# Hybrid decoder layer: the first weights' first half is loaded ahead of x's second tile, which PE turns between the first projection's products

## What is computed

```python
h = rms_norm(x, norm1_g[l])
proj = h @ w_in[l]                        # 1024 x 2856, thirteen pieces
(nq, nkc, nvc, nks, nvs, nkw, nvw, ngate, gq, gk, gv, glr, gr) = jnp.split(proj, split_points, axis=-1)
nsa_out = nsa_mixer(nq, nkc, nvc, nks, nvs, nkw, nvw, ngate, positions, ...)
gla_out = gla_mixer(gq, gk, gv, glr, gr, gla_w_gate[l], gla_b_gate[l], gla_norm_g[l])
x = x + jnp.concatenate([nsa_out, gla_out], axis=-1) @ w_out[l]
h2 = rms_norm(x, norm2_g[l])
x = x + moe_ffn(h2, w_router[l], b_router[l], w_gate_up[l], b_gate_up[l], w_down[l], b_down[l])
```

## Time and profile before

| what | value |
|---|---|
| runs | 1064.62, 1066.3, 1068.13 us, median 1066.3 |
| profiled execution | 1063.68 us, of which the span is 1061.9 us |
| PE busy in the span | 1017.3 us (96%) |
| DVE, ACT busy | 294.1 us, 168.1 us |
| HBM read | 424.83 MB, 401 GB/s over the span |
| granted TensorE clock, mean | 1.0 |

### The profile page before, as it was taken

How to read it: one execution, slowest core, us unless ns; L and a number is a source line. 1 busy time by engine, 2 the same in 40 slices (tenths; PEclk the granted TensorE clock), 3 DMA queues, 4 the chain that set the end, 5 groups by cost and what they waited for, 6 DMA issues and landing times.

```text
span 1061.9 us, 12030 instructions
## 1 busy us (share of the span) xinstructions
PE 1017.3 (96%) x4977; PEld 410.7 (39%) x4977; DVE 294.1 (28%) x681; ACT 168.1 (16%) x324; POOL 15.9 (1%) x42
## 2 busy tenths in 40 slices
PE   9999999999999999999999999999999999989998
PEld 5555644333333333333333333333333333333334
DVE  1664625222222222211222122222112222221222
ACT  2434322111111111100111011111101111110111
POOL 4100000000000000000000000000000000000000
PEclk9999999999999999999999999999999999999999
DMA  9992668999999999999999999999999999999997
GB/s 296 362 408 88 246 270 343 426 425 436 428 430 433 433 433 430 428 430 431 434 434 433 433 426 430 433 432 434 432 431 426 426 434 433 434 431 430 420 426 276
DMA packets 36023, 426.45 MB, mean 402 GB/s; under 512 B 3782, under 2 KB 12062, under 8 KB 19728
## 3 DMA queue, kind: packets, MB, share of 16 engines
q1 hardware_dynamic: 33952, 424.52, 95.0%
q0 software_dynamic: 704, 1.04, 0.5%
q10 hardware_dynamic: 1328, 0.33, 0.1%
HBM read 424.83 MB, written 1.05 MB: 401 GB/s over the span
## 4 chain that ended last, share of the span: by engine, by line
PE 62%; DMA 34%; DVE 2%; SPq 1%; issue 1%; ACT 0%; DVEq 0%
DMA pair<-in_w_down 30%; PE bank L1741 24%; PE bank L1753 14%; PE bank L1329 5%; DMA pair<-in_w_gate_up 4%; PE bank L1775 4%; PE bank L1604 3%; PE bank L1725 2%; PE bank L1767 2%; PE bank L1733 1%; PE bank L1760 1%; PE bank L1401 1%; PE bank L1969 1%; SPq L369 1%; PE bank L1361 1%; PE bank L1388 1%
## 5 line engine op out<-in xcount | busy, mean ns | idle before, releaser
L1741 PE MATMUL bank<-pair,xs 128*64 128x512 f32 x2048 | 450.1, 594 | 21.0 <-DMA pair<-in_w_gate_up 19.9
L1741 PEld LDWEIGHTS bank<-pair,xs 128*64 128x64 f32 x2048 | 143.0, 137 | 323.1 <-issue 286.9
L1753 PE MATMUL bank<-pair,sig 128*64 128x512 f32 x960 | 212.2, 593 | 14.2 <-DMA pair<-in_w_down 14.2
L1222 DVE COPY gu<-bank 128x512 f32<-128x512 f32 x32 | 36.9, 1154 | 415.3 <-PE bank L1741 415.3
L1753 PEld LDWEIGHTS bank<-pair,sig 128*64 128x64 f32 x960 | 72.3, 137 | 149.9 <-issue 143.8
L760 ACT COPY gu<-bank 128x512 f32<-128x512 f32 x32 | 36.9, 1152 | 458.1 <-PE bank L1741 458.1
L862 DVE TENSOR_TENSOR xs<-bank,gt 128x512 f32<-128x512 f32 x31 | 21.4, 691 | 221.0 <-PE bank L1733 221.0
L1329 PE MATMUL bank<-stage,xt 128*128 128x512 f32 x160 | 72.2, 598 | 0.0
L1775 PE MATMUL bank<-ys,pgt 64*128 64x512 f32 x248 | 61.6, 615 | 0.3 <-ACT ys L765 0.3
L1725 PE MATMUL bank<-xr,onehot 128*64 128x512 f32 x248 | 58.5, 592 | 0.0
L765 ACT COPY ys<-bank 128x512 f32<-128x512 f32 x31 | 18.2, 586 | 206.9 <-PE bank L1753 206.9
(11 more groups left out here) (316 smaller groups left out, 496.8 us busy)
## 6 DMA issues: line engine op xcount, KB each, us to landing
pair<-in_w_gate_up SPq DMA_DIRECT2D x51, 4096.0 KB, 39.7
pair<-in_w_down SPq DMA_DIRECT2D x24, 4096.0 KB, 37.9
pair<-in_w_gate_up SPq DMA_DIRECT2D x22, 2048.0 KB, 14.7
pair<-in_w_down SPq DMA_DIRECT2D x15, 1024.0 KB, 13.3
pair<-in_w_down SPq DMA_DIRECT2D x6, 2048.0 KB, 33.0
stage<-in_w_in SPq DMA_DIRECT2D x5, 2048.0 KB, 19.2
pair<-in_w_gate_up SPq DMA_DIRECT2D x8, 1024.0 KB, 4.9
stage<-in_w_out SPq DMA_DIRECT2D x2, 2048.0 KB, 15.6
```

Of the source, the lines that this page charges most:

```text
L1222: V.tensor_copy(gu[:, 1, :].rearrange("p (i q) -> p q i", i=FQ), up_banks[1][:].rearrange("p (q i) -> p q i", i=FQ)).then_inc(s["gu_lo"], 1)
L1741: last = mm(up_banks[a][b * CAP:(b + 1) * CAP, :].rearrange("p (q i) -> p q i", i=FQ), xs[:, k, :], cols[:, b], start=k == 0, stop=k == DK ...
L1753: last = mm(down_bank[b * CAP:(b + 1) * CAP, :], actf[:, kk % FQ, kk // FQ, :], row[:, 512 * b:512 * (b + 1)], start=kk == 0, stop=kk == D ...
```

## The change

SP issues x's first tile, then the first half of the first weights, then x's second tile, then the second half. PE no longer turns x's second tile ahead of the first product: it turns it behind the first four products (tile 0, k-tiles 0 to 3). The products then go (tile 0, low half), the turning of tile 1, (tile 0, high half), (tile 1, low half), (tile 1, high half). The turned gains go through bank 6 in place of bank 4. Nothing is added or left out; the number of instructions on every engine stays as it was.

```diff
         @block.sync
         def _(sp):
-            for ti in range(NT):
+            def rows_of_x(ti):
                 sp.dma_start(xr[:, ti, :], x[0, ti * P:(ti + 1) * P, :]).then_inc(s[f"xin{ti}"], 16)
+
+            rows_of_x(0)
...
                 if i == 0:
                     sp.dma_start(dst[:, 0:4, :], src[:, 0:4, :]).then_inc(s["w_low"], 16)
+                    rows_of_x(1)
                     dst, src = dst[:, 4:DK, :], src[:, 4:DK, :]
...
             dve.wait_ge(s["g1_full"], 1)
-            V.tensor_copy(gt2[:, 0:DK], banks[4][:, 0:DK]).then_inc(s["g1t"], 1)
+            V.tensor_copy(gt2[:, 0:DK], banks[6][:, 0:DK]).then_inc(s["g1t"], 1)
...
-            for ti in range(NT):
+            def x_turned(ti):
                 pe.wait_ge(s[f"xin{ti}"], 16)
...
-                if ti == 0:
-                    pe.wait_ge(s["grows1"], 16)
-                    tp(banks[4][:, 0:DK], grows[:], ident[0:DK, 0:DK]).then_inc(s["g1_full"], 1)
+
+            x_turned(0)
+            pe.wait_ge(s["grows1"], 16)
+            tp(banks[6][:, 0:DK], grows[:], ident[0:DK, 0:DK]).then_inc(s["g1_full"], 1)
...
-            for half in range(2):
+            def first_project(ti, half):
+                pe.wait_ge(s["xt"], 2 * ti + half + 1)
+                for k in range(4 * half, 4 * half + 4):
+                    last = mm(banks[PROJ_BANKS[ti]][:, 0:280 + RANK], xt[:, k, ti * P:(ti + 1) * P],
+                              front_slot(0)[:, k, :], start=k == 0, stop=k == DK - 1)
                 if half:
-                    front_arrived(pe, 0)
-                else:
-                    pe.wait_ge(s["w_low"], 16)
-                for ti in range(NT):
...
+                    last.then_inc(s["proj_full"], 1)
+
+            pe.wait_ge(s["w_low"], 16)
+            first_project(0, 0)
+            x_turned(1)
+            front_arrived(pe, 0)
+            first_project(0, 1)
+            first_project(1, 0)
+            first_project(1, 1)
```

More of the change, by code:

```diff
@@ L1392, in _ @@
             pe.wait_ge(s["g1t"], 1)
-            for half in range(2):
-                if half:
-                    front_arrived(pe, 0)
-                else:
-                    pe.wait_ge(s["w_low"], 16)
-                for ti in range(NT):
[L1399 to L1404, removed]
+            def first_project(ti, half):
[3 more added lines that the diff above has]
+                              front_slot(0)[:, k, :], start=k == 0, stop=k == DK - 1)
+                if half:
+                    last.then_inc(s["proj_full"], 1)
[6 more added lines that the diff above has]
+            first_project(1, 1)
             pe.wait_ge(s["xt"], 4)
```

## The result

The changed kernel takes 1070.38 us (median of 6 runs, 1069.65 to 1070.68) against 1066.34 us before (6 runs, 1064.33 to 1068.13): a ratio of 1.0042, 95% interval 1.0028 to 1.0055. It is slower by about 4 us, where 0.4 was forecast, and lies above the forecast's range. The profiled execution took 1070.55 us, of which the span is 1068.6.

A forecast was written before the change was run, and what follows sets the result against it. PE was taken to bound the kernel (busy 96%, 62% of the chain). Start -0.69 and transposes +1.10 give +0.41 us, so the median goes from 1066.3 to 1066.7 us, range 1063.9 to 1069.6.

The forecast's parts named there:

- What bounds the kernel: Whole kernel: PE, busy 96% and 62% of the chain, sets the pace; delay in the first projection carried nearly one to one.
- the delay is swallowed: Rival, behind the first projection: a later DMA or engine wait absorbs the 0.41 us, median stays 1066.3; chance 0.14.
- Part 1: Weights' first half, no longer queued behind x's second tile, lands 1.38 us sooner, near 6.66 instead of 8.04 us.
- Part 2: First product starts at 7.55 us instead of 8.24, set by DVE's scaled half of x: 0.69 us sooner.
- the 16 columns take the place of the weights: Rival at the first product: columns still land at 7.76, start 7.8 to 7.95, sum +0.74 (1067.0 us); chance 0.2.
- The clock: Rival in the first projection: TensorE falls to the lower clock, loses 2.35 us, +2.8 in all (1069.1); chance 0.04.
- Part 3: The 8 transposes of x's second tile, now between products, cost 1.10 us (bounds 0.95 to 1.30).
- Part 4: Rest of the first projection: DVE's norm chain ends near 14.2 instead of 11.75, ACT's first copy no later; costs nothing.
- The sum: First projection ends at 16.86 us, 0.41 later (bounds +0.18 to +1.01); median 1066.7 us.

The follow-up runs named there:

- cols_split: Changed kernel, first four products 280 wide without awaiting the 16 columns, added later by products with a start of their own; 1067.09 us, ratio 1.0018.
- swap_warm: Changed kernel, with ACT issuing the 16 columns ahead of the gains and 5 identity transposes filling PE's hole; 1066.41 us, ratio 1.0015 to the kernel before.
- cols_swap: Changed kernel, with ACT issuing the 16 columns ahead of the gains, 0.64 us sooner; 1067.21 us, ratio 1.0008 to the kernel before.
- cols_split2: Changed kernel, first four products 280 wide, the 16 columns' later products continuing the bank's group without a start of their own; 1066.44 us, ratio 1.0016.
- pe_only: Kernel before with only PE's order changed (x's second tile turned behind the fourth product), SP's order as before; 1067.57 us, ratio 1.0015.
- after_again: The changed kernel once more, nothing altered, for a second trace; 1070.77 us, ratio 1.0052 to the kernel before.
- before: The kernel before the change, unaltered, in its first trace; median 1066.34 us.
- sp_only: Kernel before with only SP's order changed (x's first tile, weights' first half, x's second tile, second half); 1069.10 us, ratio 1.0021.

## Why the prediction was wrong

**What bounds the kernel, and that a delay here is carried one to one:** right. The rival "the delay is swallowed" falls by the table.

**Part 1, the transfer:** right in kind. The weights landed at 6.1 instead of 6.66. I had counted nothing for the issue 0.47 us sooner, and that is most of the difference of 0.58.

**Part 2, the start: this is the step that failed.** It read: "I expect these pieces to go with the weights' first half and to land between 6.4 (as much sooner as the weights) and 7.76 (as now)". They landed at 10.07. The upper end was taken from the kernel before as if "as now" were the worst case. But "as now" was itself a product of the order that the edit changes: the columns had been issued ahead of the weights, and 666 of their pieces passed in half a microsecond in which SP's queue moved 71. I saw the rush and gave as its cause that x's tiles had gone; the second half of the observation, SP's 71 packets, was in the same view and I did not read it. The rival "the 16 columns take the place of the weights" named the right last arrival and had 0.2, but it kept the columns at 7.76: its price of 0.74 came from the same false bound, and that the edit itself could delay them was in no branch. With nothing but the columns' landing corrected, the sum would have been +1.87 + 1.10 = +3.0. The bound on the other side, no start before 7.47, did not hold either: `cols_split` started at 7.12 and `swap_warm` at 7.39, since a clock that is up earlier shortens the 8 transposes of x's first tile (1.55 and 1.87 us in place of 1.97).

**The clock, the second step that failed:** it was put at nothing in the sum and given 0.04 as a rival, and it is +1.95 of the 4.69. The rival's own price, 2.35, was near. What was wrong is the chance: I argued from a hole growing from 0.70 to 1.0 us, and did not ask what a longer one would do if the columns were late. The two rivals were priced as if independent, and the first brings about the second. The picture was off too: in the changed kernel the clock did not fall in the hole, it had not yet risen. The work that stood there before, the turning of x's second tile, was moved behind it. With a hole of 1.08 us, the forecast's own case, the clock was low in two traces of three (`cols_swap`, `cols_split2`; not `cols_split`), so the 0.41 us of the forecast was the sum at a clock that nothing secured.

**Part 3, the transposes:** 1.10 forecast, 0.87 in the chain at the higher clock, and 1.71 at the lower (`pe_only`, `after_again`). My lower bound, 0.95, was too high for the first and my upper, 1.30, too low for the second.

**Part 4:** DVE and ACT: right in that they ended later and nobody on the chain noticed, since PE was later still. ACT's first copy, said to be no later than it was, came at 18.39 instead of 14.58 and waited for DVE's factor.

**The sum and the range:** against the forecast's +0.41, the start gave 10.11 - 7.55 = +2.56 more, the clock +1.95 and the transposes 0.87 - 1.10 = -0.23, which is the measured +4.69. The range's upper end should have been 1066.3 + 1.01 + 2.5 = 1069.8 by its own terms and not 1069.6; the measured median lies above both.

Where the 4.69 us go is shown by traces in both directions: taking the columns' delay away brings the end from 21.15 to 19.55, filling the hole brings it to 19.37, both bring it to 16.47. The two steps, 1.60 and 1.78, add up to less than the 4.68 of both, since in `cols_swap` the moved transposes ran at the lower clock as well. What the edit gains by itself, 0.69 us of start, it gives back in transposes that were free before. Not shown: why the small pieces pass so fast when they are issued ahead of the weights; the issue order fits all traces here, but no run moved the issue times alone by small steps or kept the order and changed the pieces around them. Open as well are the medians of the variants, that of `swap_warm` above all.

## What to carry to other kernels

Before moving a transfer forward, list every other transfer that its first reader waits for, on other queues too, and ask in which order they are issued then; a small transfer of tiny pieces can owe its landing to that order, and the worst case for it is not "as now". Work that sits in a wait can be free twice, as x's second tile was here: it cost no time, and the clock came up during it, so moving it out of the wait cost its own duration, in one trace at the dearer pace, plus the clock on what followed. When two rivals share a cause, price them together.

## What the runs showed of the hardware

- A difference of 0.64 us in issue moved the landing of 64 KB in 64-byte pieces from 10.07 to 4.8 us. From 5.5 to 8 us in the changed kernel the two queues moved nearly equal numbers of packets (481 of 64 bytes beside 495 of 1120 bytes or 4 KB); from 5 to 5.5 us they did not (314 and 97).
- The printed granted clock is 1.00 in the first microseconds of every trace, also where like instructions run at half the later pace (0.246 against 0.138 us), and in the changed kernel up to 14 us: the trace's record begins with the first rise. At a program's start the pace is the surer witness.
- The same small pieces put in line ahead of 560 KB in one queue brought the big transfer in at 8.62 us, against 6.1 without them; 0.46 of this is its later issue.
- TensorE's clock rose after nothing but transposes: at 6.4 us in `before`, 5.4 in `sp_only`, 5.3 in `cols_split`, each time with PE busy on transposes from 1.60 us on but for 0.2 to 0.4 us. This speaks against the sentence of the Trainium skill (TensorE: Matmul & The Clock Gate, Part 4: PE-mode transpose) that transposes do not count as other work does.
- Holes of 1.08, 1.80, 2.35, 3.75 and 4.15 us ahead of the first products, with the clock not yet up, were followed by 8 rows at the lower level; 0.38, 1.14 and 1.98 us behind filler transposes were not. Not every hole of 1.08 us cost it: `cols_split` had one and ran at 0.265 us a row, its clock having risen ahead of the hole. And in `sp_only` a clock that was up fell between two holes of 1.57 and 1.44 us.
